# One product of 320 columns ahead of whole units behind paired units, sums and spreads

## What is computed

```python
def first_block(x, ...):
    for l in range(DEPTH):
        mix = hybrid_mixer(x, w_in[l], ...)      # one wide projection, two attentions, a short convolution, merge
        x = layer_norm(ALPHA * x + mix, ln1_g[l], ln1_b[l])
        ffn = swiglu(x, w_ffn_gate[l], w_ffn_up[l], w_ffn_down[l])      # 1024 -> 2816 -> 1024
        x = layer_norm(ALPHA * x + ffn, ln2_g[l], ln2_b[l])
    return x

def second_block(x, c, ctx, ...):                # a latent stream h and a context stream hc, 256 tokens each
    for l in range(DEPTH):
        h, hc = h + HALF * gt1 * swiglu_2(ada_norm(h, ...)), hc + HALF * cgt1 * swiglu_2(ada_norm(hc, ...))
        # mixing: convolution module, latent attention, Fourier mix, three gates, w_out
        h = h + gt2 * y                          # hc too, but in the last layer
        h = h + HALF * gt3 * swiglu_2(ada_norm(h, ...))                 # hc too, but in the last layer
    return rms_norm(h, g_final)
```

## Time and profile before

| what | value |
|---|---|
| median of 3 runs | 3002.68 us (3001.75 to 3007.31) |
| the profiled execution | 3005.68 us |
| its span, first to last instruction | 3003.9 us |
| granted TensorE clock, mean | 0.987 of full speed |
| PE busy | 2897.1 us, 96% |
| DVE, ACT, POOL busy | 2051.9, 1366.5, 153.3 us (68%, 45%, 5%) |
| read from memory | 482.66 MB, 161 GB/s over the span |
| chain that ended last | PE 82%, DVE 9%, ACT 4% |

### The profile page before, as it was taken

How to read it: one execution, slowest core, us unless ns; L and a number is a source line. 1 busy time by engine, 2 the same in 40 slices (tenths; PEclk the granted TensorE clock), 3 DMA queues, 4 the chain that set the end, 5 groups by cost and what they waited for, 6 DMA issues and landing times.

```text
span 3003.9 us, 59994 instructions
## 1 busy us (share of the span) xinstructions
PE 2897.1 (96%) x23648; PEld 2789.5 (93%) x23648; DVE 2051.9 (68%) x3323; ACT 1366.5 (45%) x2212; POOL 153.3 (5%) x222
## 2 busy tenths in 40 slices
PE   8999999999999999999999999999999999899998
PEld 8889999888999999998889999999999999779998
DVE  4658786658678777778764476867768566876655
ACT  5555445555446432354544354223542235545543
POOL 0000000000000000010000020000200001000000
PEclk9999999999999999999999999999999999999999
DMA  6435764435666565552212354544645445225454
GB/s 235 146 115 187 243 235 163 149 108 176 211 210 198 193 222 194 177 184 67 81 45 89 105 185 161 206 156 171 208 162 207 144 152 187 64 82 192 161 184 138
DMA packets 148053, 487.54 MB, mean 162 GB/s; under 512 B 16400, under 2 KB 25872, under 8 KB 147728
## 3 DMA queue, kind: packets, MB, share of 16 engines
q1 hardware_dynamic: 126688, 407.22, 41.0%
q0 software_dynamic: 21168, 77.60, 7.6%
HBM read 482.66 MB, written 1.05 MB: 161 GB/s over the span
## 4 chain that ended last, share of the span: by engine, by line
PE 82%; DVE 9%; ACT 4%; issue 3%; DMA 2%; POOL 0%; DVEq 0%; ACTq 0%; SPq 0%; POOLq 0%
PE bank L2042 23%; PE bank L2043 22%; PE bank L2044 22%; DVE wlo L1141 3%; ACT whi L606 2%; PE bank L1960 2%; PE bank L1961 2%; PE bank L1962 2%; DVE acc L1742 2%; PE aux L2269 1%; PE bank L2287 1%; DMA bbb<-in_w_ada 1%; PE bank L2120 1%; DMA raw<-in_w_stream 1%; DMA big<-in_w_ada 1%
## 5 line engine op out<-in xcount | busy, mean ns | idle before, releaser
L2042 PE MATMUL bank<-uhi,whi 128*128 128x256 f32 x4968 | 1397.0, 281 | 9.6 <-DVE wlo L1141 6.0
L2044 PE MATMUL bank<-uhi,wlo 128*128 128x256 f32 x4968 | 1381.1, 278 | 0.0
L2043 PE MATMUL bank<-ulo,whi 128*128 128x256 f32 x4968 | 1380.9, 278 | 0.0
L1141 DVE TENSOR_TENSOR wlo<-raw,whi 128x1024 fp32r<-128x1024 f32 (+4 forms) x850 | 951.0, 1121 | 370.7 <-ACT whi L606 362.2
L2042 PEld LDWEIGHTS bank<-uhi,whi 128*128 128x128 f32 x4968 | 935.1, 188 | 28.2 <-issue 22.9
L606 ACT CAST whi<-raw 128x1024 fp32r<-128x1024 f32 (+4 forms) x850 | 811.5, 961 | 282.7 <-PE bank L2044 179.3
L2043 PEld LDWEIGHTS bank<-ulo,whi 128*128 128x128 f32 x4968 | 934.8, 188 | 3.4 <-issue 3.0
L2044 PEld LDWEIGHTS bank<-uhi,wlo 128*128 128x128 f32 x4968 | 937.7, 189 | 0.0
L2042 PE MATMUL bank<-yhi,whi 128*128 128x256 f32 x1740 | 494.1, 284 | 16.2 <-DVE wlo L1141 8.5
L2043 PE MATMUL bank<-ylo,whi 128*128 128x256 f32 x1764 | 491.3, 279 | 0.0
L2044 PE MATMUL bank<-yhi,wlo 128*128 128x256 f32 x1740 | 484.5, 278 | 0.0
(11 more groups left out here) (297 smaller groups left out, 2939.0 us busy)
## 6 DMA issues: line engine op xcount, KB each, us to landing
raw<-in_w_stream SPq DMA_DIRECT2D x674, 512.0 KB, 3.7
big<-in_w_ada POOLq DMA_DIRECT2D x64, 512.0 KB, 3.6
vt<-in_w_ada POOLq DMA_DIRECT2D x51, 512.0 KB, 3.7
raw<-in_w_stream SPq DMA_DIRECT2D x80, 256.0 KB, 2.7
raw<-in_w_stream SPq DMA_DIRECT2D x48, 384.0 KB, 3.1
bbb<-in_w_ada POOLq DMA_DIRECT2D x29, 512.0 KB, 4.7
raw<-in_w_stream SPq DMA_DIRECT2D x32, 192.0 KB, 2.4
raw<-in_w_stream SPq DMA_DIRECT2D x16, 128.0 KB, 2.0
```

The lines of the kernel that those rows point to most:

```text
L1141: ve.tensor_tensor(wlo[:, u % SLOTS, 0:n], raw[:, u % SLOTS, 0:n], whi[:, u % SLOTS, 0:n].bitcast(F32), ALU.subtract).then_inc(s_low, 1)
L2042: te.matmul(out_, whi[:, u % SLOTS, w], hi(k)[:, cols], start=k == 0, stop=False)
L2043: te.matmul(out_, whi[:, u % SLOTS, w], lo(k)[:, cols], start=False, stop=False)
L2044: ins = te.matmul(out_, wlo[:, u % SLOTS, w], hi(k)[:, cols], start=False, stop=k == plan.kt[u] - 1)
```

## The change

A set `uneven` is kept while the program of PE is written out. `two_units`, `two_units_normed`, `by_token`, `spread`, `add_up` and the end of the attention of the first block put a word into it. The next unit that is not paired and not `fresh` issues, behind its waits and ahead of its own products, one further product: the first 128 columns of its own `whi` slot as weights, 160 columns of the moving operand read twice, so 320 columns, into its own PSUM bank with `start=True, stop=True`. The unit's first product starts its accumulation anew. The set is then cleared. Where the next unit stands in a hardware loop, the product stands once, ahead of the loop, behind the waits of the loop's first unit. The `bm` stages clear the set and get none.

```diff
+            uneven = set()
+
             def two_units(u, hi, lo, c0, c1, late=8, from_=split):
+                uneven.add("two units")
...
             def two_units_normed(u, hi, lo, c0, c1):
+                uneven.add("two units")
...
             def by_token(src, t0, t1, from_=dop):
+                uneven.add("sums by token")
...
             def spread(bank_, diagonal):
+                uneven.add("spread")
 
                 dop.wait(1)
                 te.matmul(bank_, ones, diagonal, start=True, stop=True).then_inc(s_mean, 1)
+
+            def evened(u, hi, c0):
+
+                uneven.clear()
+                wide = hi(0)[:, c0:c0 + 160].unsqueeze(1).to_broadcast([P, 2, 160])
+                te.matmul(banks[u % SLOTS][:, 0:320].rearrange("p (a b) -> p a b", a=2),
+                          whi[:, u % SLOTS, 0:P], wide, start=True, stop=True)
...
                 elif plan.freed(u):
                     pe.wait_ge(s_free[u % SLOTS], plan.freed(u) + per // SLOTS * i)
+                if uneven and not paired and not fresh and isinstance(i, int):
+                    evened(u, hi, c0)
                 for a in range(c0, c1, S):
...
                     first = 1
+                elif uneven:
+                    pe.wait_ge(s_low, u0 + 1)
+                    pe.wait_ge(s_free[u0 % SLOTS], plan.freed(u0))
+                    evened(u0, lambda k: hi(0, k), c0)
 
                 def body(i):
...
                     pe.wait_ge(*after(U[f"merge{l}"] + i))
+                uneven.add("attention")
                 stream(U[f"merge{l}"], 24, 12, lambda j, k: y1(4 * (j % 3) + k)[0],
...
             def add_up(bank_, n, c0, src):
+                uneven.add("sums over tiles")
...
+                uneven.clear()
                 stream(U[f"bm{l}"], 4 * DT, 8, rows(0), rows(1), c0, T2)
```

## The result

The kernel after takes 3030.95 us (median of 5 runs, 3021.73 to 3035.6), beside 3001.75 us for the kernel before (5 runs, 2999.21 to 3007.31): a ratio of 1.0089, 95% interval 1.0066 to 1.0112. The change makes the kernel slower by 27 to 29 us. The forecast was 2988 us, in a range from 2979 to 3012.

The account below looks back on a forecast made before the run. PE's stream of products was taken as the bound. Fast pace −26.3, added products +9.3 and waits +2 gave −15 us, so 3002.68 became 2988 us; the 8-in-10 range was 2979 to 3012 us.

Parts of the forecast that it names:

- five 512-column openings go on at the fast pace: Openings of two units passing without a wait into 256-column units: all five in the trace continue at the fast pace.
- a product wider than 256 leaves the stream fast: At the 65 places, a 320-column product was to choose the fast pace, turning 30 slow stretches fast for 26.3 us.
- The argued reason: PE's weight loads beside products: a longer product lets the next load finish and stand ready; argued only, no size of its own.
- only the cost: Rival at all 65 places: the product ahead doesn't choose the pace, products just cost 9.3 us; 3012 us, chance 0.12.
- the wrong pace: Rival: stepping from 320 to 256 columns leaves streams slow; some 6700 fast products lose 30 us; 3042 us, chance 0.09.
- The cost of a product: On PE's stream: each 320-column product costs 0.143 us, 65 of them 9.3 us, bounded by 7.3 and 15.1 us.
- The gain: 30 slow stretches behind the added products, 696.91 us long, were to shrink by 3.8%, or 26.3 us.
- ±5 us: Waits that are left choose their pace anew; allowed for in the range, with nothing put into the sum.
- the first case: Fast pace at nearly all of the 65 places: 2979 to 2996 us, chance 0.66.
- The short wait at 284 us: Ahead of the 171.65 us slow stretch: PE's 0.02 us wait was to vanish behind the product's 0.14 us delay.
- half of it: Rival: fast only at some places, or the stretches behind 284 and 2812 us stay slow; 3000 us, chance 0.13.
- The waits that take gain back: DVE waits for `in_w_ada` loads, then PE for `wlo`; gains before such waits are used up, 2 us taken off.

Follow-up runs that it names:

- w512: The kernel after with the added product 512 columns wide instead of 320, at the same 65 places; 3031.06 us, ratio 1.0122.
- after_again: The kernel after, unchanged, profiled once more; 3038.55 us in a single run.
- before_again: The kernel before, unchanged, profiled once more; 2995.55 us in a single run.
- w256: The kernel after with the added product 256 columns wide instead of 320, at the same 65 places; 3015.96 us, ratio 1.0052.
- w384: The kernel after with the added product 384 columns wide instead of 320, at the same 65 places; 3001.87 us, ratio 1.0004.
- few384: The kernel after with 384-column products at only twelve of the 65 places; 3002.07 us, ratio 1.0000.
- sums_only: The kernel after without the marks of the openings and the attention, leaving 32 products of 320 columns; 3023.05 us, ratio 1.0089.
- w384_again: Repeat of w384, 384 columns at all 65 places, for one more profile; 3009.31 us in a single run.
- pick384: The kernel after with 384 columns, without the attention and all sums by token but one, plus eight products in the bm loops; 2999.27 us, ratio 0.9991.

## Why the prediction was wrong

**The step that failed** is the one from "five 512-column openings go on at the fast pace" to "a product wider than 256 leaves the stream fast". The five cases are rows of 512-column products, followed by 256; the change puts one single 320 between products of 256. No row of the kernel before shows that, in 31 of the 36 openings. It turned a fast stream slow in 12 of 13 places. The extrapolation wasn't even safe at the width it came from: one single product of 512 among those of 256 turned a fast stream slow 12 of 12 times (w512).

**The argued reason** (the load has room behind a wide product, and the next weights stand ready) falls with it. By it 512 columns would be best, 448 better than 384, and 320 at least harmless. What chooses the pace instead stays open. The runs show only that it depends on the width and the kind of place, repeatably for streams that come fast out of an opening and behind spreads, and that it holds until the next break.

**The rivals.** I gave "only the cost" 0.12 and "the wrong pace" 0.09. The second names the effect rightly for openings: a step from 320 to 256 columns leaves the stream slow. Its size of 39 us was too high, since it took all 6700 fast products to be lost and nothing to be won: 5116 were lost (22.7 us) and 2551 won (11.3 us), behind spreads and sums by token, of which 20 of 25 went on fast, and behind 8 of the 15 openings that came in slow. Not all of that is the product's doing: waits draw the pace too, and after_again beside before_again won 1732 only. The evidence given for this rival, ten of eleven slow behind one-column products, was the right warning: an unlike product can set either pace. The first, that the product ahead chooses nothing, falls by w256 against w384: same places, 4542 slow products apart. The Trainium skill, page "TensorE: Matmul & The Clock Gate", section "Back-to-back issue gap", whose rule stood behind that rival, gives one distance for each width. That section of the Trainium skill calls its formula that of an isolated product, and says that in a stream of loads and products both set the spacing; these streams are of the second kind, which the prediction passed over. The rows of after show 0.14 us for 320 columns (333.11 to 333.25) and of w384 0.18 us for 384 (1879.61 to 1879.79), somewhat above the 136 and 163 ns that its formula gives as an estimate; of the two paces at 256 columns, which decide this case, it gives neither. The same section of the Trainium skill has about 131 ns for 512 columns in a stream of loads and products; the trace disagrees, with two distances in 0.46 us.

**The cost of a product** was sized right: 0.143 us forecast, 145 ns measured behind openings at the fast pace and 147 behind those at the slow pace. The sum of 9.3 us stands beside 9.8 measured net, or 9.3 when the shorter waits ahead of the merge stages are taken off.

**The gain** of 26.3 us had the wrong sign in the trace: a loss of 11.4 us, with 2531 more slow products, not some 5900 fewer. It was oversized for a second reason: the profiled execution of before, at 7559 slow products, had more of them than the next one (5394), and the stretch at 284.40 us, a quarter of the sum, was fast there with no change at all. A pace behind a wait can't be won by a change ahead of it for sure. I had put ±5 us for this; single executions of before alone spread over 36 us. The ends of 2979 and 2996 us for the first case don't follow from the terms given for them either: with the 2 us of waits and both ends of the cost these come to 2977 and 2998.

**The short wait at 284 us** did vanish, as said: the added product starts at 283.96 us and the unit follows at 0.14 and then 0.12, 0.12 us, with a fast stream until 300.32. There a wait of 1.94 us took its place. Behind it came the half clock up to 306.6 us and then the fast pace again, not the slow one that "half of it" expected; the slow pace begins at the next added product, at 333.11 us. **The waits that take gain back** were right in kind, and 2 us was too small: all waits together took 4.6 us in after and 4.0 in w384. PE's waits for `wlo` at the unit's first product rose from 14.8 us to 19.0 us,

```profile
PE bank L2057 <- DVE wlo L1141: 19.0, 26, 2.7
```

and in few384 to 22.5 us; in before_again they are 17.3, so a part of this is chance. Half clock stands behind some of these waits only: behind the one of 1.94 us above, but not behind one of 1.33 us that ends at 327.5 us. That clock was in no step of the sum.

**What stays open.** w256 leaves nearly every stream behind an opening as it came in, in both of its profiles, and its products cost 7.8 us net; its profiles are 3000.9 and 3005.9 us long. Yet its median is 3015.96 us, 17 above before and 7 above what was expected. The profiled executions of w256 and sums_only lie at the low end of their runs, so the slower ones may hold more slow products; no trace here shows it.

## What to carry to other kernels

Measure the distance from start to start over long stretches before you trust that PE is at its peak: here 4% lay between two paces with the same clock and no wait. Don't set a pace with a product whose width you have only seen in another setting; try the very width at the very place, and expect one that works at openings to fail behind a sum. And before counting a gain from one profile, take a second of the same kernel: what stands behind a wait may be drawn anew, and what is won there may be spent at the next load that DVE waits for.

## What the runs showed of the hardware

- Products of 256 columns with a weight load each run at 113.3 or 117.8 ns from start to start at a granted clock of 1.00, for up to 1569 products in one stretch; no stretch held a pace between them.
- A single product of another width in between can turn it: behind openings of 256, 128, 320 and 512 columns turned a fast stream slow (14 of 14, 12 of 13, 12 of 12) and in part a slow one fast (8 of 12; 8 of 15, but 2 of 15 in the second profile; 13 of 16); 352, 384 and 448 always left it fast there. Behind spreads 384 was fast 14 of 14 times in each of w384 and w384_again and 13 of 14 in pick384, and 352 slow 14 of 14.
- One more product of 320 columns in a stream at the full clock costs 141 to 152 ns net, behind openings, spreads and sums alike.
- One program ran from 2987.9 to 3024.2 us on a single core, and two of its traces, 10.2 us apart, differ by 2165 products of the slow pace, 9.6 us.
